# Hybrid decoder trunk: one-half pieces turned in the other PSUM bank, an even filling of four steps a block, and the first two output matmul groups inside the last attention block

## What is computed

```python
proj = h @ w_in
gq, gk, gv, gr, ga, dq, dk, dv = jnp.split(proj, IN_SPLITS, axis=-1)
o_g = gla_chunked(gq, gk, gv, log_a)
o_g = rms_norm(o_g, gla_norm) * silu(gr)
# differential attention, per head and block of 128 queries, causal
s = einsum(q, k) * scale + bias          # two maps m = 0, 1
p = softmax(s)
a = p[0] - lam * p[1]
o_d = a @ v
o_d = rms_norm(o_d, diff_norm) * (1 - lam_init)
return concatenate([o_g, o_d]) @ w_out
```

## Time and profile before

| | |
|---|---|
| median of 3 runs | 2565.43 us (2564.73 to 2567.64) |
| profiled execution | 2565.14 us, span of its trace 2563.3 us |
| PE busy | 2448.2 us, 96% of the span |
| DVE, ACT, POOL busy | 1541.9, 965.6, 184.2 us |
| attention stretch, layer 0, 285 to 515 us | PE busy 204.21 of 230 us |
| attention stretch, layer 1, 1540 to 1770 us | PE busy 202.81 of 230 us |

### The profile page before, as it was taken

One profiled execution on the slowest core, in us unless ns is written; L12 is line 12 of the kernel. 1 busy time (PEld: TensorE's weight loads), 2 busy tenths in 40 slices (PEclk: granted clock), 3 DMA queues, 4 the chain that ended last, 5 costly groups with the idle time before them and its releaser, 6 DMA issues. The chain is left out here.

```text
span 2563.3 us, 30636 instructions
## 1 busy us (share of the span) xinstructions
PE 2448.2 (96%) x11778; PEld 1971.6 (77%) x11778; DVE 1541.9 (60%) x2509; ACT 965.6 (38%) x1763; POOL 184.2 (7%) x241
## 2 busy tenths in 40 slices
PE   6999899899999999999989998898999999999997
PEld 5788676688788888888768886667888888887876
DVE  5655566557877776545652555666586666653554
ACT  5212345544322222344543123545443333333443
POOL 1001100021000000101100010000200000001000
PEclk8999999999999999999999998999999999999999
DMA  7631200131544443565522112001323232237544
GB/s 268 222 107 34 58 9 25 34 107 66 170 159 149 155 148 99 199 218 169 186 92 66 36 40 42 25 34 42 111 71 99 74 95 79 75 125 262 186 148 141
DMA packets 220033, 283.50 MB, mean 111 GB/s; under 512 B 10719, under 2 KB 171376, under 8 KB 218864
## 3 DMA queue, kind: packets, MB, share of 16 engines
q1 hardware_dynamic: 197648, 200.77, 24.7%
q0 software_dynamic: 22240, 80.77, 9.0%
HBM read 244.00 MB, written 37.50 MB: 110 GB/s over the span
## 5 line engine op out<-in xcount | busy, mean ns | idle before, releaser
L2596 PE MATMUL ps<-hT,wsp 128*128 128x512 f32 x1440 | 333.6, 389 | 2.6 <-issue 2.6
L2147 PE MATMUL ps<-hT,wsp 128*128 128x512 f32 x736 | 307.7, 418 | 14.0 <-DVE F L1614 14.0
L2596 PEld LDWEIGHTS ps<-hT,wsp 128*128 128x128 f32 x1440 | 270.0, 188 | 59.9 <-issue 4.1
L2149 PE MATMUL ps<-hT,wsp 128*128 128x512 f32 x736 | 293.2, 398 | 0.0
L2148 PE MATMUL ps<-hT,wsp 128*128 128x512 f32 x736 | 293.0, 398 | 0.0
L2478 PE MATMUL ps<-wsp,asp 128*128 128x512 f32 x1080 | 254.7, 392 | 3.3 <-DVE asp L1908 3.0
L2478 PE MATMUL ps<-hT,asp 128*128 128x512 f32 x1032 | 245.2, 394 | 4.7 <-DVE asp L1908 4.6
L2478 PEld LDWEIGHTS ps<-wsp,asp 128*128 128x128 f32 x1080 | 202.1, 188 | 49.5 <-issue 5.1
L2596 PE MATMUL ps<-tsum,wasp 128*128 128x512 f32 x960 | 233.3, 400 | 0.0
L2478 PEld LDWEIGHTS ps<-hT,asp 128*128 128x128 f32 x1032 | 194.1, 189 | 49.9 <-issue 4.6
L2596 PEld LDWEIGHTS ps<-tsum,wasp 128*128 128x128 f32 x960 | 184.3, 193 | 40.9 <-DVE wasp L1967 0.3
(11 more groups left out here) (261 smaller groups left out, 3848.6 us busy)
## 6 DMA issues: line engine op xcount, KB each, us to landing
raw<-in_w_down SPq DMA_DIRECT2D x100, 512.0 KB, 3.6
F<-in_w_mod SPq DMA_DIRECT2D x80, 512.0 KB, 4.8
raw<-in_w_in SPq DMA_DIRECT2D x48, 512.0 KB, 3.8
raw<-in_w_gate_up SPq DMA_DIRECT2D x48, 512.0 KB, 4.9
F<-in_w_gate_up SPq DMA_DIRECT2D x40, 512.0 KB, 5.6
acts_d<-F POOLq DMA_DIRECT2D x38, 512.0 KB, 6.5
F<-acts_d POOLq DMA_DIRECT2D x38, 512.0 KB, 5.3
out_x<-W POOLq DMA_DIRECT2D x32, 512.0 KB, 3.4
```

The costliest lines, as they stand in the source:

```text
L2147: mm(o, a(0), b(0), start=start, stop=False)
L2149: return mm(o, a(1), b(0), start=False, stop=stop)
L2596: last = mm(bank(j, p), block_of(p, z)[:, k * P:k * P + P], times(p, zz, k), start=p < B_A22 and k == 0 and z == 0 and zz == 0, stop=k == ...
```

## The change

1. `STEPS` gives four fill steps to every block, two before and two behind the transposes (three in blocks 4 to 7 of head 0, five in most of head 3).
2. The turning is cut into 14 pieces of one half (`PIECES`: eight `o` of the GLA outputs, six `v` of values). Piece i is turned by PE at the middle (k = 4) of half i of the filling, in the bank that this half does not use, and copied out by DVE behind that block's `maxes` (`piece_out`). `bank_free(i)` is what `fill` waits for at the start of a half: the copy of piece i - 1.
3. The values of head 0 are turned in the last GLA tile ahead of its last four fill steps, and copied out there; DVE's first `maxes` stand ahead of that tile's low part and its last product; ACT's `column_out(7)` stands ahead of the square of tile 7.
4. In the first block of heads 1 to 3 the first fill steps stand ahead of `weighted(h - 1, 7)`.
5. `hi_out` and `lo_out` of k = 0, 1, 2 move from blocks 0 to 2 of head 3 to blocks 2 to 4. In the last block token tile 0 is multiplied for k = 0 and k = 1 (`out_first`), and `oT_hi(1)` stands ahead of the copies of that block's probabilities.

```diff
-STEPS = (((3, 3), (3, 3), (0, 0), (0, 2), (3, 3), (3, 3), (2, 0), (0, 0)),
-         ((0, 2), (0, 3), (3, 0), (3, 3), (3, 2), (3, 2), (3, 2), (3, 0)),
-         ((0, 2), (0, 3), (3, 0), (3, 3), (3, 2), (3, 2), (3, 2), (3, 0)),
-         ((0, 3), (3, 2), (3, 2), (3, 2), (3, 2), (3, 3), (3, 0), (0, 0)))
+STEPS = (((2, 2), (2, 2), (2, 2), (2, 2), (2, 1), (2, 1), (2, 1), (2, 1)),
+         ((2, 2), (2, 2), (2, 2), (2, 2), (2, 2), (2, 2), (2, 2), (2, 2)),
+         ((2, 2), (2, 2), (2, 2), (2, 2), (2, 2), (2, 2), (2, 2), (2, 2)),
+         ((2, 2), (3, 2), (3, 2), (3, 2), (3, 2), (3, 2), (3, 0), (0, 0)))
+PIECES = (("o", 0, 0), ("v", 1, 0), ("v", 1, 1), ("o", 0, 1), ("o", 1, 0), ("o", 1, 1), ("o", 2, 0),
+          ("v", 2, 0), ("v", 2, 1), ("o", 2, 1), ("o", 3, 0), ("v", 3, 0), ("o", 3, 1), ("v", 3, 1))
...
+                column_out(NT - 1)
                 gla_square(NT - 1)
                 hi(l, N_COL + NT + 1)
-                column_out(NT - 1)
...
+                        if h == HEADS - 1 and b == NT - 1:
+                            oT_hi(1)
                         for g in range(groups_before(b + 1) - groups_before(b)):
                             probs(b, g)
...
-                            if b < 3:
-                                hi_out(b)
+                            if b in (2, 3, 4):
+                                hi_out(b - 2)
...
                     if t + 1 < NT:
                         gla_gates(t + 1)
+                    else:
+                        values_out(0, 0, 0)
+                        values_out(0, 1, 1)
...
+                    if t + 1 == NT:
+                        dve.wait_ge(s_bias, l * 16 + 16)
+                        maxes(0, 0, 0)
+                        maxes(0, 0, 1)
                     lo_sums(N_COL + t + 2)
...
-                        if b == 0 and h:
-                            values_out(h, 0)
-                        if b == 0 and h:
-                            values_out(h, 1)
+                        for i in pieces_turned(h, b):
+                            piece_out(i)
...
-                        if h == 0 and b in (2, 3, 7):
-                            gated({2: 0, 3: 1, 7: 3}[b])
...
-                            elif f in (8, 10, 12, 14):
-                                pe.wait_ge(s_ve, (l * HEADS + f // 2 - 4) * 2 + hf + 1)
-                            elif f == 9:
-                                pe.wait_ge(s_sr, l * 10 + 2 + hf + 1)
                             else:
-                                pe.wait_ge(s_fe, evacuated(l, f - 1, hf))
+                                bank_free(i)
+                        if late and k == 4 and i < len(PIECES):
+                            turn_piece(i)
...
+                    if t == NT - 1:
+                        turn_values(0, 0, 0)
+                        turn_values(0, 1, 1)
                     fill(16 * t + 12, 16 * t + 16)
...
-                        if b == 0 and h:
-                            turn_values(h, 0)
-                            turn_values(h, 1)
-                        if h == 0 and b in (2, 3):
-                            to_features(b - 2)
                         if b:
                             weighted(h, b - 1)
-                        elif h:
+                        fill(a, a + STEPS[h][b][0])
+                        if b == 0 and h:
                             weighted(h - 1, NT - 1)
-                        fill(a, a + STEPS[h][b][0])
+                        if h == HEADS - 1 and b == NT - 1:
+                            out_first(0)
                         turned(h, b, 0)
                         if b >= 4:
                             turned(h, b, 1)
-                        if h == 0 and b in (6, 7):
-                            to_features(b - 4)
                         fill(a + STEPS[h][b][0], a + sum(STEPS[h][b]))
+                        if h == HEADS - 1 and b == NT - 1:
+                            out_first(1)
                         if b == NT - 1:
                             turned(h, b, 2)
...
-                    for t in GROUPS[0]:
+                    for t in GROUPS[0][1 if k < 2 else 0:]:
```

More of the change, by code:

```diff
@@ L94, in steps_before, with pieces_turned @@
         sum(p) for p in STEPS[h][:b]) + (STEPS[h][b][0] if part else 0)
+def pieces_turned(h, b):
+    a = steps_before(h, b, 0)
+    return [i for i in range(len(PIECES)) if a <= 8 * i + 4 < a + sum(STEPS[h][b])]
 def halves_ended(h, b):
@@ L1555, in own_mod_columns, with values_out, maxes @@
                     dve.wait_ge(s_par, 3)
+                def values_out(h, g, bank):
+                    dve.wait_ge(s_vt, (l * HEADS + h) * 2 + g + 1)
+                    o = Fv[h % 2] + HALF * g
+                    v.tensor_copy(F[:, o:o + HALF], ps[:, bank, :]).then_inc(s_ve, 1)
+                def maxes(h, b, m):
+                    at, n = l * 64 + h * 16 + 2 * b + m, (b + 1) * P
+                    w = min(n, NEAR)
+                    dve.wait_ge(s_qk, 1 + at + 1)
+                    near = pair(1 + m)[:, n - w:n]
+                    o = h * NEAR + NEAR - w
+                    v.tensor_tensor(near, near, bias[:, o:o + w], ALU.add).then_inc(s_ba, 1)
+                    dve.wait_ge(s_ba, at + 1)
+                    v.tensor_reduce(ast[:, A_NM + 2 * b + m:A_NM + 2 * b + m + 1],
+                                    pair(1 + m)[:, 0:n], AX.X, ALU.max, negate=True
+                                    ).then_inc(s_mx, 1)
                 def gla_tile(t):
@@ L1608, in _, with piece_out, gated @@
                         own_mod_columns()
[L1610 to L1616, removed]
+                def piece_out(i):
+                    kind, h, g = PIECES[i]
+                    if kind == "v":
+                        values_out(h, g, 1 - i % 2)
+                    else:
+                        gated(h, g, 1 - i % 2)
+                def gated(h, g, bank):
                     if h < 2:
                         dve.wait_ge(s_gr, l * HEADS + h + 1)
[L1620 to L1628, removed]
+                    dve.wait_ge(s_of, l * 8 + 2 * h + g + 1)
+                    o = F[:, Fsr + S * h + HALF * g:Fsr + S * h + HALF * g + HALF]
+                    if h < 2:
+                        v.scalar_tensor_tensor(o, ps[:, bank, :], cur[:, P_GN:P_GN + 1], o,
+                                               ALU.mult, ALU.mult).then_inc(s_sr, 1)
+                    else:
+                        v.tensor_scalar(o, ps[:, bank, :], cur[:, P_GN:P_GN + 1], None, ALU.mult
+                                        ).then_inc(s_sr, 1)
                 def gated_last(h):
@@ L1647, in oT_lo @@
                                                ALU.subtract).then_inc(s_ol, 1)
[L1649 to L1660, removed]
                 def combine(h, b):
@@ L2398, in _ @@
                     last.then_inc(s_gO, 1)
-                def to_features(h):
-                    pe.wait_ge(s_gG, 1 + l * NT + NT)
-                    for g in range(2):
-                        if h % 2:
-                            pe.wait_ge(s_sr, l * 10 + 2 * (h - 1) + g + 1)
-                        else:
-                            pe.wait_ge(s_fe, evacuated(l, 8 + h // 2, g))
-                        for t in range(4 * g, 4 * g + 4):
-                            o = Fgv + 512 * t + DV * h
-                            last = nc.tensor.transpose(ps[:, g, t % 4 * P:t % 4 * P + P],
-                                                       F[:, o:o + DV], ident)
-                        last.then_inc(s_of, 1)
                 def scores(h, b):
@@ L2491, in out_tile, with out_first @@
                                  lambda zz, k, h: wres(k, zz)[:, 512 * h:512 * h + 512], ks, KT - 1)
+                def out_first(k):
+                    split(N_OUT + k)
+                    pe.wait_ge(s_ol, 1 + l * 8 + k + 1)
+                    if k == 0:
+                        pe.wait_ge(s_fe, evacuated(l, 15))
+                    out_tile(0, (k,))
                 def head(h):
@@ L2530, in _ @@
                 pe.wait_ge(s_ex, 1 + l * 64 + 64)
-                pe.wait_ge(s_fe, evacuated(l, 15))
                 for k in range(KT):
```

51 lines of the change are left out of this document (33 added, 18 removed).

## The result

The changed kernel takes 2522.36 us (median of 4 runs, 2521.5 to 2523.39), the kernel before 2565.08 us in 4 runs (2562.05 to 2567.64). The ratio is 0.9834, with a 95% interval of 0.9817 to 0.9851: faster by 43 us. The forecast was 2537 us with a range from 2517 to 2553. Sign and range held. The gain was forecast as 28.6 us; it is 42.7 us between the medians and 42.6 between the two profiled executions (spans 2563.3 and 2520.7 us).

The account below looks back on a forecast made before the run. PE's work at its granted clock plus its idle time was taken as the bound. From 2565.14 us, 20.6 of idle time and 8 of clock would go, 28.6 in total, giving 2537 us, range 2517 to 2553.

Parts of the forecast that it names:

- Places and idle time: PE's waits in the two attention stretches, counted block by block: 53.0 us falls to 32.4, a gain of 20.6.
- The chains: Scores to next scores where a filling tile ends: 7.5 us in head 0 block 3, 8.0 in heads 1 and 2 block 4.
- The clock: Half-rate windows in the attention stretches: 14.4 us lost before, four short windows losing 6 remain, so 8 come back.
- first two: Half-rate windows of 6.8 us in the attention stretches, said to begin when PE had been idle 1.62 and 3.10 us.
- case A: Whole kernel: bank waits and head 0's idle time go, waits at tile ends stay; 2530 to 2545 us, 62%.
- rival B: Attention stretches: tile ends are hidden too, 56 us gained, 2509 us, or 2523 halfway; 13%.
- The start and the last block: Each layer: second scores 5.5 us earlier, at 294.4 in layer 0; last block's idle time 3.1 us instead of 4.6.
- Part 4: First block of heads 1 to 3: `weighted` behind the fill makes exponentials 1.4 us later but adds nothing to the time.
- The bank waits: The filling's waits for DVE's value copies: 7.0 us a layer go, since copies hide beside ACT's last exponential.
- C: Half rate follows many new 2 us waits: 2548 us with seven long windows, 2566 with one behind each of 14 waits; 14%.
- D: Attention blocks: the filling's waits for copies hide scores waits of the same length; gain 3 us, 2562 us, 6%.
- E: Every attention block: the scores chain becomes longer than four steps; slower, 2585 us at 1.2 us longer, 5%.

Follow-up runs that it names:

- the kernel with the late low part: The changed kernel with DVE's low part of a weight made one block later, behind that block's maxima instead of ahead of `combine`: 2505.85 us, ratio 0.9773.
- the old table: The changed kernel with `STEPS` as in the kernel before and all else as after the change: 2548.19 us, ratio 0.9933.
- part 2 alone: The kernel before with the turning in 14 half pieces, old steps, start and last block, but `hi_out` and `lo_out` moved: 2567.22 us, ratio 1.0016.
- the version with all low parts late: The changed kernel with the low parts of the weights and of head 3's output weights one block later on DVE: 2501.66 us, ratio 0.9758.

## Why the prediction held, and what it mis-sized

**Places and idle time: right.** Every place that it named has its wait in the trace, ended by what it said. For layer 0, in us:

| place | forecast | measured |
|---|---|---|
| start | 1.1 | 0.97 |
| head 0, block 3 | 2.2 | 0.52 + 1.33 |
| head 0, block 5 | 0.3 | 0.24 |
| heads 1, 2, block 4, each | 2.2 | 0.22 + 1.61 |
| heads 1 to 3, block 0, each | 0.6 | 0.53 |
| head 3, blocks 4 and 5 | 1.3, 2.0 | 1.07, 1.71 |
| last block | 3.1 | 2.80 |
| `weighted`, three places | none | 0.38, 0.13, 0.13 |
| sum | 16.2 | 14.56 |

The chains were sized well: scores to scores is 7.5 us in head 0 and 8.01 in head 1 (360.38 to 368.39), against 7.5 and 8.0. So was the work: "5.3" and "5.85" in these blocks, and 5.36 and 5.89 us from scores to scores in the kernel with the late low part, where they have no wait. A block of 8.01 us thus loses 2.12 us to its waits, near the forecast 2.2, while the trace calls 1.83 of it idle. Most of the rest is shown as busy: between fill matmuls without a wait one starts every 0.23 us though each is shown as 0.39 us long, and the last one before a wait shows all its 0.39. That accounts for the rows of head 0's block 3 (2.14 lost, 1.85 idle) and of heads 1 and 2. Head 3's waits came out 0.2 and 0.3 us shorter than forecast, and 0.64 us of `weighted` waits were left out. In all, idle time fell by 23.9 us instead of 20.6.

**The clock: the term that was mis-sized.** "Four, 6 us, so 14.4 - 6 = 8 us come back." None remained in the attention stretches, so all 14.4 us came back, and 3.5 more elsewhere: 17.9 instead of 8. The waits "near 2 us" that were to bring four windows measured at most 1.71 us. How the clock went with such waits can be counted over the attention stretches of all twelve traces of this case. A window was counted when it began in the wait or at most 2.4 us behind it:

| waits of PE, us | with a half-rate window |
|---|---|
| one of 1.3 to 1.72, none longer beside it | 0 of 51 |
| one of 1.88 to 1.96 | 3 of 7 |
| one of 2.50 or 2.51 | 11 of 12 |
| two close together: 1.62 and 3.10, 2.23 and 2.10 or 2.46, 1.40 and 2.46 | 14 of 14 |
| 3.01 and 1.61 | 0 of 1 |

The prediction's reason, that the long windows stood where "two long waits came close together", does not hold in general: the window of the last block stands beside a single 2.50 us wait (with 1.25 us ahead of it and 0.36 and 0.46 behind), and with the old table the window at 310.06 begins inside the first wait of its pair (308.22 to 310.45). The reading under it was off too: of the "first two" windows only the one at 292.17 stands at the earlier trace rows; the one at 316.06 stands at waits of 1.40 and 2.46 us in head 0.

Was it luck? In part. The measured 2522.36 us lies outside case A's own 2530 to 2545. The stated range held it because it reached down to 2517 for half of rival B, whose mechanism did not happen. Of the 14 us by which the gain was larger, 9.9 are this clock term and 3.3 the idle time; both erred the same way.

**Which price the clock has.** The prediction took half of PE's busy time in the half-rate windows. Over the whole span that is (82.12 - 46.37) / 2 = 17.9 us, and with 24.3 us of idle time 42.2 of the 42.6 us. The Trainium skill (TensorE: Matmul & The Clock Gate, Terms) charges half of the throttled time, (95.60 - 51.18) / 2 = 22.2, which would make 46.5. The measurement sides with the prediction's way: idle time inside such a window is not lost twice.

**The start and the last block: right.** 5.5 us earlier was forecast for the second scores, and 6.1 is measured. The moved output matmuls took away 1.7 us of idle time a layer (1.5 was forecast) and left no wait behind.

**Part 4: right**, nothing.

**The bank waits: right in the sum, wrong as a reason by themselves.** "The copies cost nothing, and the waits of 7.0 us a layer go" holds in the changed kernel, and part 2 alone is worth nothing. The gain is that of table and pieces together. The prediction's sum never depended on which part it came from, because it counted idle time block by block.

**The rivals.** B (tile ends hidden) didn't happen, but the reason given against it, that "the chain of the earlier trace rows has no slack in it", was wrong: moving `lo` behind the maxima takes every one of those waits away. C (half rate behind many waits) failed in the changed kernel and shows with the old table (10.7 us in four windows). D holds for part 2 alone only. E failed: no ordinary block has a wait for its scores, apart from 0.24 us.

**Open.** What decides on a half-rate window: a wait of 1.88 us brought one and waits of 3.01 and 1.61 us didn't, in one kernel, one execution, and of six waits of 1.90 or 1.96 us in the kernel before two did. Every 2.50 us wait had shorter ones near it, so single waits and groups are not told apart. What the even table is worth without the pieces. Why the half-rate windows outside the attention stretches vary, 46.4 us of PE work after, 53.3 before, 50.4 in the version with all low parts late, isn't known: their code is the same. Another order on ACT, the next thing to try on the three `weighted` waits, which end with its copies (`probs`), wasn't run.

## What to carry to other kernels

When filler work is spread over a chain that another pair of engines sets, give every link the same filling and look at what else stands in those engines' queues. In an in-order queue the place of one 1.2 us conversion step, ahead of the chain's instruction or beside another engine's part of it, was worth 16.5 us over 12 such conversions (13.9 of them seen as idle time). Removing a wait is worth only what isn't waiting right behind it, as part 2 alone shows. And a long wait can cost twice, in idle time and in clock: here waits of 2.50 us nearly always did and those up to 1.72 us with none longer beside them never, so shorten the longest waits first.

## What the runs showed of the hardware

- The granted clock stayed at 1.00 through about ten waits of up to 1.71 us a layer and, once, through 3.01 and 1.61 us with 2.1 us of work between them. It fell to 0.50 once 1.2 us behind a wait of 1.88 us, and beside 11 of 12 waits of 2.50 or 2.51 us.
- A block with waits of 0.22 and 1.61 us took 8.01 us and the same block without them 5.89: 2.12 us lost, 1.83 of them shown as idle.
- PE's busy time less half of that in half-rate windows is 2407.1 us before and 2406.7 after, and 2406.3 with part 2 alone (2455.7 - 98.78 / 2) and with the old table (2442.1 - 71.55 / 2). Over all twelve traces it lies between 2404.4 and 2407.1, while the spans run from 2500.3 to 2571.3 us: half rate and idle time explain all but some 3 us of what differs.
